# First MLP layer by seven block products for pairs of channel tiles, in a transformer-like layer kernel on one core

## The chip, the core and the metric

The kernel runs on one core of a Trainium2 chip. The core has TensorE for matrix products, VectorE, ScalarE and GpSimd for element-wise work, SyncE that issues the DMAs, an on-chip memory SBUF of 128 partitions and a small accumulator memory PSUM, into which TensorE writes. The engines run their own instruction lists side by side and wait for each other by semaphores. In the rows they are called PE (PEld is its weight load), DVE, ACT, POOL and SP.

The metric is the device time of one launch in microseconds (us). Three runs of the kernel before took 1729.58, 1735.76 and 1736.58 us; the median is 1735.76.

## The reference

One layer on 1024 tokens of width 1024, in float32. The time mixer before it fills the first thousand us and isn't touched. What matters here is the second half:

```python
x = _layernorm(DEEPNORM_ALPHA * x + g1 * mix, ln1_g, ln1_b)
h = _modulate(x, sh2, sc2)                       # layer norm, times (1 + sc2), plus sh2
ff = jnp.square(jax.nn.relu(h @ w_ff1 + b_ff1)) @ w_ff2 + b_ff2     # 1024 -> 4096 -> 1024
return _layernorm(DEEPNORM_ALPHA * x + g2 * ff, ln2_g, ln2_b)
```

To keep float32 accuracy with bf16 matmuls, every operand is split in a high part (its bf16 rounding) and a low part (the residual, rounded). A product is three matmuls: high x high, high x low, low x high.

## The kernel before

The work is written as a chain of stages, each a block with one list per engine and a barrier at its end. Two stages matter.

**The output stage, `phase_out`.** It goes over eight token tiles `t` of 128 tokens. TensorE makes the output projection (`out_products`, L2015), VectorE and ScalarE add the residual and normalise twice, TensorE transposes the result (L2383), ScalarE applies scale and shift by eighths (`piece`, L2271), rounds to `a_hi` (L2275), and GpSimd makes the residual `a_lo` (`low`, L2247). So `a_hi` and `a_lo` hold the input of the MLP with channels on the partitions: 8 channel blocks of 128 by 1024 tokens. For the last tile VectorE does half of the piece (L2367, L2370) and the residual. At the end TensorE already makes the tiles 0 and 1 of the MLP's 4096 hidden channels (`ff_part`, L2206), for the tokens whose pieces are ready; their last 128 tokens wait for the last `a_lo`. The weights of tiles 2 and 3 are loaded and split here too (L150, L154).

**The MLP stage, `phase_mlp`.** The 32 tiles of hidden channels go in 8 groups of four. For a tile TensorE issues 8 channel blocks x 3 matmuls x 2 halves of the tokens, 48 matmuls of 128x512 (`gemm_rows`, L218), into a PSUM tile of 1024 columns. ScalarE takes the relu (L2515), VectorE the square (L2607), ScalarE rounds to `c_hi` (L2519), GpSimd makes `c_lo` (L2552). Beside it the weights of the tile after next are loaded (512 KB), rounded by ScalarE (L2437) and their residual made by GpSimd (L2441). For a group the second layer's weights (2 MB) are loaded, scaled by VectorE (L2599), rounded (L2524) and their residual made (L2557). TensorE's order is: first layer of group i+1, then second layer of group i, 16 outputs of 12 matmuls (`gemm_tokens`, L674), each added by VectorE to the sum in SBUF (L2619). In the last group VectorE and ScalarE normalise what is done. The middle of the stage stands in engine loops (`steps`), each turn of which does two groups. The order on each engine is the order of the code.

Of the kernel before, what the change touches and what calls it, by code (L numbers as in the profile page):

```python
# [7 lines left out]
F32 = mybir.dt.float32  # L8
# [2200 lines left out]

def phase_out(nc, g, a):  # L2210

    with ExitStack() as es:
        sb = lambda n, s=(P, D), d=F32: es.enter_context(nc.sbuf_tensor(f"ou_{n}", list(s), d))
        names = "vec brow mm y s1 v1 sd1 r1 n1 gain bias keep s2 v2 sd2 r2 n2 turn hf hi lo tail_hf tail_hi".split()
# [4 lines left out]
        hf = sb("hf", (P, KT, P))  # L2219
# [5 lines left out]
        turned = [es.enter_context(nc.psum_tensor(f"ou_turned{u}", [P, D], F32)) for u in range(2)]  # L2225
# [7 lines left out]
        load_next, split_next, cut_next, _ = first_weights(nc, "ff1", ff_buffers(g), lambda u, i: [(slice(0, KT), w1[:, :, (2 + u) * P:(3 + u) * P])])  # L2233
        tok = lambda t: slice(t * P, (t + 1) * P)
        inside = lambda t: 0 <= t < TT
        LAST = TT - 1
# [7 lines left out]
        def low(eng, t):  # L2244
            if inside(t):
                wait(eng, t, "hi")
                eng.tensor_tensor(g.a_lo[:, :, tok(t)], hf[:], g.a_hi[:, :, tok(t)], ALU.subtract).then_inc(s["lo"], 1)  # L2247

        @block.sync
        def _(sp):  # L2250
# [7 lines left out]
            wait(sp, LAST, "mm")  # L2258
            load_next(sp)

        @block.scalar
        def _(act):

            def piece(t):
# [23 lines left out]
            for t in range(TT):  # L2288
# [9 lines left out]
                root(t, 1)  # L2298
            second(LAST)
            for u in range(2):  # L2300
                split_next(act, u)
            piece(LAST)

        @block.gpsimd
        def _(pool):
            for t in range(TT):
                low(pool, t - 2)
                if t in SPLIT_AT:
                    cut_early(pool, t - SPLIT_AT[0])
            low(pool, LAST - 1)  # L2310
            for u in range(2):
                cut_next(pool, u)

        @block.vector
        def _(dve):
# [45 lines left out]
            scale(LAST, 1)  # L2361
            keep(LAST)
            wait(dve, LAST, "turn")
            wait(dve, LAST - 1, "lo")
            half = KT // 2
            for kt in range(half, KT):
                dve.tensor_scalar(hf[:, kt, :], turned[LAST % 2][:, kt * P:(kt + 1) * P], g.ada[:, ADA["sc2"] + kt:ADA["sc2"] + kt + 1],  # L2367
                                  g.ada[:, ADA["sh2"] + kt:ADA["sh2"] + kt + 1], ALU.mult, ALU.add).then_inc(s["tail_hf"], 1)
            dve.wait_ge(s["tail_hf"], half)
            dve.tensor_copy(g.a_hi[:, half:KT, tok(LAST)], hf[:, half:KT, :]).then_inc(s["tail_hi"], 1)  # L2370
            dve.wait_ge(s["tail_hi"], 1)
            low(dve, LAST)

        @block.tensor
        def _(pe):
# [33 lines left out]
            ff_part(pe, ps[1], early[1][1], early[2][1], g, HALF, SEQ - P)  # L2409
            wait(pe, LAST, "lo")  # L2410
# [4 lines left out]
def ff_buffers(g):  # L2415

    tile = lambda at: g.z[:, at, :].rearrange("p (k n) -> p k n", n=P)
    part = lambda at, x: g.z[:, at, x * HALF:(x + 1) * HALF].bitcast(BF16).rearrange("p (k n) -> p k n", n=P)
    return [tile(10 + u) for u in range(2)], [part(12 + u, 0) for u in range(2)], [part(12 + u, 1) for u in range(2)]


def ff_weights(nc, g, a):


    ff = Net()
    w1 = a["w_ff1"][0].rearrange("(k p) n -> p k n", p=P)
    stage, ff.hi, ff.lo = ff_buffers(g)
    loaded, hi_ready, ff.lo_ready, ff.used = ([nc.alloc_semaphore(f"ff1_{n}{u}") for u in range(2)] for n in "in hi lo used".split())

    def load(sp, m, u, col):  # L2430
        sp.wait_ge(ff.lo_ready[u], m + 1)
        sp.dma_start(stage[u], w1[:, :, ds(col, P)]).then_inc(loaded[u], 16)

    def split_hi(act, m, u):
        act.wait_ge(loaded[u], (m - 1) * 16)
        act.wait_ge(ff.used[u], m + 1)
        act.activation(ff.hi[u], stage[u], ACT.Copy).then_inc(hi_ready[u], 1)  # L2437

    def split_lo(pool, m, u):
        pool.wait_ge(hi_ready[u], m - 1)  # L2440
        pool.tensor_tensor(ff.lo[u], stage[u], ff.hi[u], ALU.subtract).then_inc(ff.lo_ready[u], 1)  # L2441

    ff.load, ff.split_hi, ff.split_lo = load, split_hi, split_lo
    return ff


def phase_mlp(nc, g, a, out):

    with ExitStack() as es:  # L2452
# [4 lines left out]
        w2 = a["w_ff2"][0].rearrange("(g k p) n -> p (g k) n", p=P, k=GT)  # L2457
        st2 = sb("st2", [P, GT, D])
        hi2, lo2 = ([sb(f"{n}{b}", [P, GT, D], BF16) for b in range(2)] for n in ("hi2_", "lo2_"))
        r = [sb(f"r{u}", [P, SEQ]) for u in range(2)]  # L2460
        ps1 = g.ps
        wide = [es.enter_context(nc.psum_tensor(f"ff_ps2_{u}", [P, D], F32)) for u in range(2)]
        ps2 = [wide[u // 2][:, u % 2 * HALF:(u % 2 + 1) * HALF] for u in range(4)]
        ff = ff_weights(nc, g, a)
        s_used1 = ff.used
# [259 lines left out]
```

## Time and profile before

| what | us |
|---|---|
| median of three runs | 1735.76 |
| span of the profiled execution | 1730.9 |
| runs, lowest and highest | 1729.58, 1736.58 |
| TensorE busy in the span | 1643.6 |
| VectorE, ScalarE, GpSimd busy | 769.0, 562.3, 451.3 |

The profiled execution gives a span, from its first to its last instruction; no device time of its own stands beside it, so the 4.9 us between its span and the median of the runs are taken as what lies around it. A matmul of 128x512 is shown with 0.38 us, but the next one starts before it ends, so a stretch of matmuls is read by its starts. An element-wise operation that is held up while it runs is shown longer: its span holds the wait. In a merged row (x4) the span covers all of them.

### The profile page before, as it was taken

The page shows a single profiled execution, that of the slowest core. Times are in us where ns is not written, and L with a number is a line of the kernel's source. Part 1 is how long each engine was busy: PE and PEld are TensorE (multiplying, and loading weights), DVE is VectorE, ACT ScalarE, POOL GpSimd, SP SyncE. Part 2 cuts the span into 40 slices and gives each one's busy share as a digit, 9 for nine tenths or more (in the row PEclk, how much of TensorE's full clock was granted, in tenths as well). Part 3 has the DMA queues.
Part 4 walks back from the last instruction along what each step waited for, and adds up shares of the span by engine and source line. Part 5 has one row for each costly group of instructions (what it writes and reads, how often), then busy time and mean ns, then how long its engine had stood idle before and what let it go on. Part 6 is the DMA issues. An engine that isn't in the chain of part 4 may idle for free. (4 is left out here: it accounts for less than half of the span.)

```text
span 1730.9 us, 34492 instructions
## 1 busy us (share of the span) xinstructions
PE 1643.6 (95%) x14983; PEld 857.5 (50%) x15178; DVE 769.0 (44%) x1061; ACT 562.3 (32%) x884; POOL 451.3 (26%) x236
## 2 busy tenths in 40 slices
PE   4998999998999998999999999999999999999997
PEld 2444666666545555544444455444444444444443
DVE  5597666666325455313111486433232323232338
ACT  5323544454324555411312165421211212120300
POOL 1231322222110112123422122742323333232310
PEclk9999999999999999999999999999999999999999
DMA  9851001000111200312110311420202021112002
GB/s 354 265 199 41 16 4 39 4 28 28 27 46 28 62 1 1 126 58 61 48 36 25 110 49 47 137 86 25 73 24 73 25 72 36 61 36 85 1 1 97
DMA packets 105773, 109.69 MB, mean 63 GB/s; under 512 B 2592, under 2 KB 82610, under 8 KB 105394
## 3 DMA queue, kind: packets, MB, share of 16 engines
q1 hardware_dynamic: 105648, 107.82, 19.2%
q8 instruction: 103, 1.69, 0.4%
q14 instruction: 22, 0.18, 0.0%
HBM read 101.52 MB, written 4.19 MB: 61 GB/s over the span
## 5 line engine op out<-in xcount | busy, mean ns | idle before, releaser
L218 PE MATMUL tokens_ps<-a_hi,z 128*128 128x512 bf16 x878 | 228.5, 379 | 0.9
L674 PE MATMUL ff_ps<-ff_hi,c_lo 128*128 128x512 bf16 x503 | 190.6, 379 | 0.6
L674 PE MATMUL ff_ps<-ff_hi,c_hi 128*128 128x512 bf16 x501 | 189.9, 379 | 1.4 <-DVE z L2619 0.9
L674 PE MATMUL ff_ps<-ff_lo,c_hi 128*128 128x512 bf16 x501 | 189.9, 379 | 0.6
L2619 DVE TENSOR_TENSOR z<-ff_ps,z 128x512 f32<-128x512 f32 x128 | 88.3, 690 | 205.0 <-PE ff_ps L674 204.3
L2515 ACT ACTIVATE ff_r<-tokens_ps,cols 128x1024 f32<-128x1024 f32 x30 | 33.4, 1114 | 421.4 <-PE tokens_ps L218 414.4
L2441 POOL TENSOR_TENSOR z<-z 128x1024 bf16<-128x1024 f32 x28 | 62.3, 2225 | 345.1 <-ACT z L2437 345.1
L218 PEld LDWEIGHTS tokens_ps<-a_hi,z 128*128 128x128 bf16 x896 | 87.6, 98 | 105.8
L2607 DVE TENSOR_TENSOR ff_r<-ff_r 128x1024 f32<-128x1024 f32 x32 | 41.1, 1284 | 219.2 <-ACT ff_r L2515 219.2
L218 PE MATMUL tokens_ps<-a_lo,z 128*128 128x512 bf16 x438 | 131.1, 379 | 0.5
L195 POOL TENSOR_TENSOR mg_wlo<-mg_stage,mg_whi 128x1024 bf16<-128x1024 f32 x21 | 45.6, 2175 | 149.9 <-ACT mg_whi L191 149.9
L2552 POOL TENSOR_TENSOR c_lo<-ff_r,c_hi 128x1024 bf16<-128x1024 f32 x32 | 75.9, 2371 | 29.4 <-ACT c_hi L2519 29.4
L674 PEld LDWEIGHTS ff_ps<-ff_hi,c_hi 128*128 128x128 bf16 x512 | 50.1, 98 | 61.6 <-issue 1.3
L674 PEld LDWEIGHTS ff_ps<-ff_hi,c_lo 128*128 128x128 bf16 x512 | 50.1, 98 | 60.4
L674 PEld LDWEIGHTS ff_ps<-ff_lo,c_hi 128*128 128x128 bf16 x512 | 50.1, 98 | 60.2
L808 DVE TENSOR_TENSOR_SCAN b_lo<-z,sb_ahead 128x256 f32<-128x256 f32 (+3 forms) x32 | 50.5, 1621 | 46.8 <-ACT z L925 46.8
L218 PEld LDWEIGHTS tokens_ps<-a_lo,z 128*128 128x128 bf16 x448 | 43.8, 98 | 52.9
L2557 POOL TENSOR_TENSOR ff_lo<-ff_st,ff_hi 128x1024 bf16<-128x1024 f32 x32 | 68.1, 2158 | 0.0
L2599 DVE TENSOR_TENSOR ff_st<-ff_st,z 128x1024 f32<-128x1024 f32 x32 | 67.3, 2160 | 1.7 <-DMA ff_st<-w_ff 1.7
L808 DVE TENSOR_TENSOR_SCAN b_hi<-z,sb_ahead 128x128 f32<-128x128 f32 (+3 forms) x32 | 48.3, 1551 | 43.1 <-ACT z L925 43.1
L2169 DVE TENSOR_TENSOR mg_ga<-mg_ga,mg_ps 128x1024 f32<-128x1024 f32 x7 | 8.5, 1221 | 131.6 <-PE mg_ps L218 131.6
L1648 PE MATMUL rw_front<-a_hi,z 128*128 128x512 bf16 x179 | 58.2, 387 | 3.0 <-issue 2.9
(420 smaller groups left out, 3219.2 us busy)
## 6 DMA issues: line engine op xcount, KB each, us to landing
ff_st<-w_ff SPq DMA_DIRECT2D x8, 2048.0 KB, 7.7
z<-w_ff SPq DMA_DIRECT2D x30, 512.0 KB, 4.0
ada_w<-w_ada SPq DMA_DIRECT2D x6, 2048.0 KB, 8.2
z<-w_in SPq DMA_DIRECT2D x18, 512.0 KB, 4.4
z<-w_ada SPq DMA_DIRECT2D x8, 1024.0 KB, 13.5
mg_stage<-w_in SPq DMA_DIRECT2D x16, 512.0 KB, 4.0
zs_stage<-w_in SPq DMA_DIRECT2D x8, 512.0 KB, 8.2
ada_w<-w_ada SPq DMA_DIRECT2D x4, 1024.0 KB, 13.5
```

Of the source, the lines that this page charges most:

```text
L195: pool.tensor_tensor(lo[u][:], stage[u][:], hi[u][:], ALU.subtract).then_inc(lo_ready[u], 1)
L218: last = pe.matmul(out[:, h * HALF:(h + 1) * HALF], w[:, kt, :], a[:, slot, h * HALF:(h + 1) * HALF], start=(x == 0 and y == 0), stop=(x = ...
L674: last = pe.matmul(out, a[:, slot, at], w[:, x, n], start=(x == 0 and y == 0), stop=(x == k - 1 and y == 2))
L808: dve.tensor_tensor_scan(prod[b][:, 0:nk][:, ::-1], m, masked, 1.0, ALU.mult, ALU.max).then_inc(s_scan, 1)
L1648: mm = pe.matmul(unit_bank(u)[:], w_part[:, kt, :], a_part[:, kt, h * HALF:(h + 1) * HALF], start=(x == 0), stop=(x == 3 * KT - 1))
L2441: pool.tensor_tensor(ff.lo[u], stage[u], ff.hi[u], ALU.subtract).then_inc(ff.lo_ready[u], 1)
L2515: act.activation(r[u][:], (wide if begun and t >= begun else ps1)[u][:], ACT.Relu, bias=g.cols[:, ds(gr * GT + (b1 + t), 1)]).then_inc(s_r ...
L2552: pool.tensor_tensor(g.c_lo[:, GT * par + t, :], r[u][:], g.c_hi[:, GT * par + t, :], ALU.subtract).then_inc(s_ulo[u], 1)
L2557: pool.tensor_tensor(lo2[par][:, k, :], st2[:, k, :], hi2[par][:, k, :], ALU.subtract).then_inc(s_o2, 1)
L2599: dve.tensor_tensor(st2[:, k, :], st2[:, k, :], g.g2, ALU.mult).then_inc(s_m2, 1)
L2607: dve.tensor_tensor(r[u][:], r[u][:], r[u][:], ALU.mult).then_inc(s_sq[u], 1)
L2619: dve.tensor_tensor(acc, ps2[x % 4], acc, ALU.add).then_inc(s_acc, 1)
```

## The change

For tile pairs the first layer is a 2x2 block product. The weights of a pair of tiles are split by input channels (blocks 0 to 3, blocks 4 to 7) and by tile, the activations by input channels and by half of the tokens. Instead of eight block products, each of 12 matmuls of 128x512, seven are made (`ff_product`), of sums of blocks on both sides, and the four quarters of the result are sums of the seven products. This holds for the tiles 2 to 31, 15 pairs; tiles 0 and 1 stay as they were.

The sums of activation blocks are made once, at the end of the output stage, on VectorE, from the float32 pieces, which for this are all kept (`piece_of`); they are rounded and split into `b_hi`, `b_lo` (`sums`, `sum_high`, `sum_low`). The sums of weight blocks are made for every pair (`ff_sums`, four additions on VectorE in a 1 MB staging buffer `st1`, of which there is one), after the unsummed blocks have been split from it (`first_high`, `first_low`) and before the summed ones are (`sums_high`, `sums_low`). The sums of products are made by VectorE from PSUM (six additions of 128x512 in `pair`), after ScalarE has copied the first product to SBUF (`u2`); relu, square and the split then go by quarters of 128x512. The products have four banks of PSUM: products 5 and 3 stand where product 1 stood, and 4 where 2 stood, so TensorE waits for the copy or the addition that empties a bank. The second layer's weights now come in halves of 1 MB. Products 1 and 2 of the first pair are made in the output stage. The engine loops are written out.

```diff
+FF_ORDER = (1, 2, 6, 7, 5, 4, 3)
+QUARTERS = ((0, 0), (1, 1), (1, 0), (0, 1))
+def ff_product(pe, g, w, n, out, onto=False):
+    whi, wlo, bhi, blo = ff_operands(g, w)[n]
+    for kt in range(PAIRS):
+        for y, (m, b) in enumerate(((whi, bhi), (whi, blo), (wlo, bhi))):
+            last = pe.matmul(out, m[:, kt, :], b[:, kt, :], ...)
+def ff_sums(eng, st, k):
+    if k == 0:
+        return eng.tensor_tensor(st[:, K1, N1], st[:, K0, N1], st[:, K1, N1], ALU.add)
...
 # output stage, VectorE
             scale(LAST, 1)
+            sums(HT)
             keep(LAST)
+            sums(HT + 1)
+            dve.wait_ge(s["wal"], 2)
+            for k in range(4):
...
+                ff_sums(dve, next_st, k).then_inc(s["ws"], 1)
             wait(dve, LAST, "turn")
...
             low(dve, LAST)
+            sums(HT + 2)
+            sums(LAST)
+            for t in range(HT + 1, TT):
+                sum_low(dve, t, 1)
 # output stage, TensorE
             ff_part(pe, ps[1], early[1][1], early[2][1], g, HALF, SEQ - P)
+            for x in range(2):
+                ff_product(pe, g, next_w, FF_ORDER[x], turned[0][:, x * HALF:(x + 1) * HALF]).then_inc(s["ahead"], 1)
             wait(pe, LAST, "lo")
 # MLP stage, VectorE
+            def pair(n, x, banks, late=None):
...
+                dve.tensor_tensor(quarter(0, 0), u2, of(2), ALU.add).then_inc(s_c, 1)
+                product(n, 6)
...
+                dve.tensor_tensor(u2, u2, of(6), ALU.add).then_inc(s_c, 1)
+                square(n, 0)
...
+                dve.tensor_tensor(u3, u2, of(7), ALU.add).then_inc(s_c, 1)
+                if late:
+                    late()
...
+                dve.tensor_tensor(quarter(1, 1), u3, of(5), ALU.add).then_inc(s_c, 1)
+                square(n, 1)
 # MLP stage, TensorE
+            def pair(n, x):
...
+                    if p == 5:
+                        pe.wait_ge(s_p1, n + 1)
+                    if p == 4:
+                        pe.wait_ge(s_c, n * 6 + C11)
+                    if p == 3:
+                        pe.wait_ge(s_c, n * 6 + C22)
```

How the instructions move shows at three places. The first is VectorE at the end of the output stage, before: L2335 stores the last row, L2367 to L2247 are the last piece.

```order
L2335 SCALAR_TENSOR_TENSOR z<-ou_y,ou_vec 128x1024
L2367 TENSOR_SCALAR ou_hf<-ou_turned,ada 128x128 x4
L2370 CAST a_hi<-ou_hf 128x4x128
L2247 TENSOR_TENSOR a_lo<-ou_hf,a_hi 128x8x128
L2212 UNCONDITIONAL_BRANCH
```

The same place of the changed kernel, from the second block of activation sums on (L2438 is the store; a first block of four stands ahead of it; L2264 to L2269 are the weight sums).

```order
L2438 SCALAR_TENSOR_TENSOR z<-ou_y,ou_vec 128x1024
L2444 TENSOR_TENSOR ou_hf<-ou_hf 128x512
L2446 TENSOR_TENSOR ou_hf<-ou_hf,ou_xf 128x512
L2448 TENSOR_TENSOR ou_xf<-ou_hf,ou_xf 128x4x128
L2450 TENSOR_TENSOR ou_xf<-ou_xf 128x4x128
L2264 TENSOR_TENSOR c_hi<-c_hi 128x4x128
L2266 TENSOR_TENSOR c_hi<-c_hi 128x4x128
L2268 TENSOR_TENSOR c_hi<-c_hi 128x4x128
L2269 TENSOR_TENSOR c_hi<-c_hi 128x4x128
L2488 TENSOR_SCALAR ou_x<-ff_wide,ada 128x128 x4
L2491 CAST a_hi<-ou_x 128x4x128
L2314 TENSOR_TENSOR a_lo<-ou_x,a_hi 128x8x128
```

Twelve sums now stand between the last normalisation and the last piece, and behind its residual follow eight more and three residuals of `b_lo`.

The second place is VectorE at the start of the MLP, before: squares and scalings of the first group, up to the start of the engine loop.

```order
L2607 TENSOR_TENSOR ff_r<-ff_r 128x1024 x2
L2599 TENSOR_TENSOR ff_st<-ff_st,z 128x1024 x4
L2607 TENSOR_TENSOR ff_r<-ff_r 128x1024 x2
L2478 UNCONDITIONAL_BRANCH
L2478 ISA
```

And now: L2860 are the squares of tiles 0 and 1, L2803 scalings, L2264 to L2269 weight sums for the second pair, L2830 the addition that frees the bank of product 2, L2814 squares of quarters, L2844 the addition that frees the bank of product 5.

```order
L2860 TENSOR_TENSOR a_hi<-a_hi 128x4x256
L2860 TENSOR_TENSOR a_lo<-a_lo 128x4x256
L2803 TENSOR_TENSOR ff_st<-ff_st,z 128x1024 x2
L2264 TENSOR_TENSOR z<-z 128x4x128
L2266 TENSOR_TENSOR z<-z 128x4x128
L2268 TENSOR_TENSOR z<-z 128x4x128
L2269 TENSOR_TENSOR z<-z 128x4x128
L2830 TENSOR_TENSOR a_hi<-ff_u,ff_wide 128x2x256
L2833 TENSOR_TENSOR ff_u<-ff_u,ff_wide 128x512
L2814 TENSOR_TENSOR a_hi<-a_hi 128x2x256
L2837 TENSOR_TENSOR ff_u<-ff_u,ff_wide 128x512
L2844 TENSOR_TENSOR a_lo<-ff_u,ff_wide 128x2x256
```

The additions on which TensorE waits stand behind scalings and weight sums, and a square stands between them.

The third place is ScalarE between the first and the second pair, which has no like in the kernel before: L2655 rounds the last quarter of the first pair, L2645 a half of the second layer's weights, L2635 to L2640 split the first-layer weights of the third pair, L2660 copies the second pair's first product.

```order
L2655 ACTIVATE c_hi<-a_hi 128x512
L2645 ACTIVATE ff_hi_0<-ff_st 128x1024 x2
L2635 ACTIVATE ff_last<-z 128x512
L2636 ACTIVATE z<-z 128x1024
L2640 ACTIVATE z<-z 128x2048
L2660 ACTIVATE ff_u<-tokens_ps 128x512
```

The copy that frees the bank of the first product stands behind all weight work for the next pair.

## Rows read from the trace of the kernel before

**Rows 1.** The page, busy time of TensorE: us, share, instructions.

```profile
PE 1643.6 (95%) x14983; PEld 857.5 (50%) x15178; DVE 769.0 (44%) x1061; ACT 562.3 (32%) x884; POOL 451.3 (26%) x236
```

**Rows 2.** Windows of the MLP stage, all engines.

```profile
core 0: us, PE busy (x) PEld busy (x) DVE busy (x) ACT busy (x) POOL busy (x), PEclk, DMA share, GB/s
1200.00:1300.00 100.00, 99.47 (x455) 45.35 (x464) 35.24 (x30) 22.49 (x22) 34.01 (x15) 1.00 0.15 48
```

**Rows 3.** TensorE's waits: line, who ended them, us, times, longest.

```profile
PE ff_ps L218 <- POOLq L88: 1.9, 1, 1.9
...
PE tokens_ps L2206 <- DVE a_lo L2247: 1.1, 1, 1.1
...
PE ff_ps L674 <- DVE z L2619: 0.9, 1, 0.9
```

**Rows 4.** Timeline of TensorE in the MLP: start, us, engine, line, operation, idle before.

```profile
1103.33 1.03 PE L218 MATMUL tokens_ps<-a_hi,z 128*128 128x512 bf16 x4
1104.19 0.59 PE L218 MATMUL tokens_ps<-a_lo,z 128*128 128x512 bf16 x2
```

**Rows 5.** Timeline of VectorE, two operations of 128x512.

```profile
961.21 0.69 DVE L2197 TENSOR_TENSOR mg_m<-mg_ga,mg_gb 128x512 f32<-128x512 f32 x1
...
1230.87 0.69 DVE L2619 TENSOR_TENSOR z<-ff_ps,z 128x512 f32<-128x512 f32 x1 [1.90 <-PE ff_ps L674]
```

**Rows 6.** Timeline of ScalarE, rounding of the second layer's weights.

```profile
1226.57 3.88 ACT L2524 ACTIVATE ff_hi<-ff_st 128x1024 bf16<-128x1024 f32 x4
```

**Rows 7.** Timeline of GpSimd in the MLP.

```profile
1229.62 8.40 POOL L2557 TENSOR_TENSOR ff_lo<-ff_st,ff_hi 128x1024 bf16<-128x1024 f32 x4
...
1287.50 2.22 POOL L2441 TENSOR_TENSOR z<-z 128x1024 bf16<-128x1024 f32 x1 [5.97 <-ACT z L2437]
1289.68 3.11 POOL L2552 TENSOR_TENSOR c_lo<-ff_r,c_hi 128x1024 bf16<-128x1024 f32 x1
```

**Rows 8.** Timeline of VectorE in the MLP, squares and scalings.

```profile
1082.16 2.25 DVE L2607 TENSOR_TENSOR ff_r<-ff_r 128x1024 f32<-128x1024 f32 x1 [2.13 <-ACT ff_r L2515]
...
1224.35 1.23 DVE L2607 TENSOR_TENSOR ff_r<-ff_r 128x1024 f32<-128x1024 f32 x1 [9.13 <-ACT ff_r L2515]
...
1287.65 8.49 DVE L2599 TENSOR_TENSOR ff_st<-ff_st,z 128x1024 f32<-128x1024 f32 x4
```

**Rows 9.** Timeline of VectorE at the end of the output stage.

```profile
1065.36 1.21 DVE L2335 SCALAR_TENSOR_TENSOR z<-ou_y,ou_vec 128x1024 f32<-128x1024 f32 x1
1068.28 1.37 DVE L2367 TENSOR_SCALAR ou_hf<-ou_turned,ada 128x128 f32<-128x128 f32 x4 [1.71 <-PE ou_turned L2383]
1069.68 0.47 DVE L2370 CAST a_hi<-ou_hf 128x512 bf16<-128x512 f32 x1
1070.76 2.46 DVE L2247 TENSOR_TENSOR a_lo<-ou_hf,a_hi 128x1024 bf16<-128x1024 f32 x1 [0.61 <-ACT a_hi L2275]
```

**Rows 10.** Timeline of TensorE between the output stage and the MLP.

```profile
1073.28 0.23 PE L2206 MATMUL tokens_ps<-a_hi,c_lo 128*128 128x128 bf16 x1 [1.14 <-DVE a_lo L2247]
...
1075.91 0.22 PE L2206 MATMUL tokens_ps<-a_hi,c_lo 128*128 128x128 bf16 x1
1078.08 0.38 PE L218 MATMUL ff_ps<-a_hi,z 128*128 128x512 bf16 x1 [1.95 <-POOLq L88]
```

**Rows 11.** Timeline of GpSimd at the end of the output stage.

```profile
1067.73 4.40 POOL L154 TENSOR_TENSOR z<-z 128x1024 bf16<-128x1024 f32 x2 [2.32 <-ACT z L150]
```

**Rows 12.** The page, DMA issues: transfer, count, KB each, us to landing.

```profile
ff_st<-w_ff SPq DMA_DIRECT2D x8, 2048.0 KB, 7.7
z<-w_ff SPq DMA_DIRECT2D x30, 512.0 KB, 4.0
```

**Rows 13.** Windows of TensorE behind a long wait: length, busy, clock, DMA share, GB/s.

```profile
676.00:680.00 4.00, 1.66 (x5) 0.54 0.00 0
680.00:684.00 4.00, 4.00 (x16) 0.61 0.00 0
```

**Rows 14.** Timeline of TensorE at the same place: the matmul behind the wait.

```profile
678.34 0.63 PE L894 MATMUL tokens_ps<-a_lo,mg_whi 128*128 128x512 bf16 x1 [5.95 <-POOL mg_wlo L154]
```

More of the change, by code:

```diff
@@ L2224, in phase_out @@
         ps = g.ps
-        turned = [es.enter_context(nc.psum_tensor(f"ou_turned{u}", [P, D], F32)) for u in range(2)]
+        turned = g.wide
         block = es.enter_context(nc.Block())
@@ L2412, in _ @@
                 ff_part(pe, ps[u], early[1][u], early[2][u], g, SEQ - P, SEQ)
[L2415 to L2444, printed above, removed]
 def phase_mlp(nc, g, a, out):
@@ new lines, in high, with pair @@
+            def high(par, x, n, k):
+                t, h = QUARTERS[k]
+                act.wait_ge(s_sq, n * 4 + k + 1)
+                act.activation(pieces(c_at(g.c_hi, par, x, t, h)), quarter(t, h), ACT.Copy).then_inc(s_uhi, 1)
+            def pair(gr, par, x, n, banks, early=None, late=None):
+                act.wait_ge(s_prod, n * NP + 1)
+                act.wait_ge(s_c, n * 6)
+                act.activation(u2, pieces(bank(banks, x, 1) if banks is narrow else banks[0]), ACT.Copy).then_inc(s_p1, 1)
+                for k in range(4):
+                    relu(gr, x, n, k)
+                    if k == 0 and early:
+                        early()
+                    high(par, x, n, k)
+                    if k == 1 and late:
+                        late()
@@ L2538, in _ @@
+            steps(first, step)
             for t in range(TT):
@@ L2543, in _ @@
         def _(pool):
-            credit(pool, ff.lo_ready * 3 + s_ulo + [s_o2])
-            def group(gr, par, last, begun=0):
-                for t in range(GT):
-                    u, m = t % 2, gr * 2 + t // 2
-                    if not (last and t >= 2) and t >= begun:
-                        ff.split_lo(pool, m + 1, u)
-                    pool.wait_ge(s_uhi[u], m + 1)
-                    pool.tensor_tensor(g.c_lo[:, GT * par + t, :], r[u][:], g.c_hi[:, GT * par + t, :], ALU.subtract).then_inc(s_ulo[u], 1)
@@ L2570, in _ @@
+            steps(first, step)
         @block.vector
@@ new lines, in first, with step, late @@
+            def first():
+                for t in range(2):
+                    dve.wait_ge(s_frelu, t + 1)
+                    dve.tensor_tensor(r[t], r[t], r[t], ALU.mult).then_inc(s_fsq, 1)
+                scale2(0, 0)
+                for k in range(4):
+                    sums(2, k)
+                pair(0, 1, ps2)
+                scale2(0, 1)
+                for k in range(4):
+                    sums(3, k)
+            def step(i, par, last, more):
+                gr = i + 1
+                if not last:
+                    scale2(gr, 0)
+                    pair(gr * 2 - 1, 0, narrow)
+                    scale2(gr, 1)
+                    def late():
+                        if more:
+                            for k in range(4):
+                                sums(gr * 2 + 2, k)
+                    pair(gr * 2, 1, narrow, late)
@@ L2621, in step @@
                         norm(t, h, i * NO + x + 2)
+                    if more and 6 <= x < 10:
+                        sums(gr * 2 + 3, x - 6)
                 if last:
@@ L2650, in second, with step @@
                                 slice(h * HALF, (h + 1) * HALF), range(GT * par, GT * par + GT)).then_inc(s_mm2, 1)
-            def step(i, par, last):
+            def step(i, par, last, more):
                 if not last:
-                    group(i + 1)
+                    pair((i + 1) * 2 - 1, 0)
+                    pair((i + 1) * 2, 1)
                 second(i, par)
-            steps(pe, lambda: group(0, 2), step)
+            steps(first, step)
 def setup(nc, es):
```

423 lines of the change are left out of this document (318 added, 105 removed).

## The prediction

> **What bounds the kernel now.** I read the page's busy shares first, then the windows, then TensorE's waits, then the timelines of the places that the change touches. TensorE is busy 95% of the span [rows 1]. In the MLP stage it is busy 99.5 of every 100 us at full clock, VectorE 35, ScalarE 22, GpSimd 34 [rows 2]. Its waits there sum to 3.9 us: 1.9 behind the barrier between the output stage and the MLP, 1.1 for the last a_lo of VectorE, 0.9 in the MLP [rows 3]. So the MLP is a dense stream of matmuls, and what counts is their start-to-start time, not the 0.38 us that one takes: four starts lie between 1103.33 and 1104.19, 0.2155 us each [rows 4]. Sums are made against this execution (span 1730.9 us) and moved to the median of the runs, 1735.8, by adding the 4.9 us between them.
>
> **What goes.** Tiles 0 and 1 stay as they are. For each of the other 15 pairs the first layer issued 96 matmuls; seven block products of 12 are 84. The instruction lists agree: 180 matmuls fewer. 180 x 0.2155 = **38.8 us less**, if the rest keeps up. A pair now takes 7 x 2.59 = 18.1 us of TensorE in place of 20.7.
>
> **What is added, and its prices.** Per pair VectorE gets six additions with one operand in PSUM (0.69 each, priced by the L2619 row), four sums of weight blocks (0.69, priced by L2197 [rows 5]), and four squares of half width for two of 1.23. ScalarE gets a copy of the first product and copies of 512 and 2048 columns (I take 0.6 and 1.9, since a run of four 1024-wide ones takes 3.88 [rows 6]). GpSimd makes the same residuals (2.1 per 1024 columns, four in 8.40 [rows 7]) in other sizes: 1.07, 2.12 and 4.2. By sums alone this fits.
>
> What does not fit so easily is that VectorE and GpSimd stop each other. GpSimd took the residual at 1287.50; VectorE's four scalings, issued at 1287.65, took 8.49 us where free operations of this width take 1.23 each, 4.9, and GpSimd's next residual, 1289.68, took 3.11 in place of 2.12 [rows 7, 8]. The additions from PSUM show none of it: 0.69 at 1230.87, in the middle of GpSimd's run of four [rows 5, 7]. So I count: an operation of VectorE with two inputs in SBUF (squares, scalings, weight sums, block sums of the activations, residuals) waits for the GpSimd operation under way, up to 1.9 us behind a 1024-wide one, up to 4 behind a 2048-wide one, and the other way round 1.0; then the two alternate. Each holds the other off some 0.1 to 0.2 us less than its own span, else the 8.49 would be 9.1 (2.07 + 1.23 + 2.12 + 3 x 1.23).
>
> The Trainium skill, "SBUF — State Buffer", "Who interferes with whom", calls this an exclusive lock between a VectorE operation with two SBUF inputs and a GpSimd operation that reads SBUF, held for the whole instruction. By that rule, the trace agrees on who waits; on how long, its 8.49 is a little short of the whole-instruction count. What the whole-instruction hold would do here is the second rival.
>
> **Step A, the end of the output stage.** In the trace VectorE stores the last row at 1065.36, waits for the last transposes until 1068.28, makes its half of the last activation piece and its residual, done 1073.22; TensorE goes on at 1073.28, ends at 1076.13, and starts the MLP at 1078.08, 1.95 later [rows 9, 10]. Now twelve sums of 0.69 stand ahead of that piece (8.3 us, plus the store 1.2: 1074.9), while GpSimd has four 2.12 residuals running; three meetings of about 1.4 make it 1079. Piece and cast, 1.9: 1081. At that moment GpSimd starts the 2048-wide residual (before it was two 1024-wide ones, 4.40, out of VectorE's way [rows 11]), so the last a_lo waits and ends at 1086. Behind it stand eight more sums (5.7), three residuals (3.5) and two meetings (3.8): VectorE is through at 1099. The barrier adds 1.95: TensorE starts the MLP at 1101. It has done two products ahead (5.2). Loss: 1101 - 1078.1 - 5.2 = **17.7 us**. Bounds: 6.8 without any meeting, 20 with whole-instruction holds.
>
> **Step B, the first pair.** Counted from TensorE's start at 1101. The products 6, 7 and 5 end at 7.8. Product 4 writes the bank that holds product 2, so it waits for the first addition, which stands on VectorE behind two squares, two scalings and four weight sums. Those need a 1 MB load (between 4.0 for 512 KB and 7.7 for 2 MB [rows 12]; I take 4.7), two copies (1.7) and two residuals (3.2). From 5 to 20 GpSimd has d_lo, a_lo, two c_lo and two second-layer residuals in a row, 11.7 us, with VectorE's two scalings and first three sums each one behind a GpSimd operation. The first addition comes at 20.5, product 4 at 21.2: **13.4 lost**. Product 3 accumulates onto product 5's bank and waits until the fourth addition has read it; ahead of that is a square that meets the 4.2 us residual of the weight sums: **5.0 lost**. Bounds for both: 6.6 and 20.
>
> **Step C, the second pair.** TensorE has products 1, 2, 6, 7 done at 41.9. Product 5 waits until ScalarE has copied product 1 out, and on ScalarE this copy stands behind all of the weight work for the third pair. That has one staging buffer, which is free at 27, and ScalarE comes to it only behind the first pair and the second-layer copies, at 39; then copies 1.7, four GpSimd operations to 46, four sums 2.8, the 1.9 copy, the copy itself: 50.8. **9.0 lost** (bounds 8 to 10).
>
> **Step D, the third pair.** Four weight sums stand inside the chain of additions, behind two residuals that start after the first addition; **4.1 lost** (bounds 1.8 to 6).
>
> **Step E, groups after that, six of them.** The two pairs take 36.2 us of TensorE. In that time the shared port is wanted for 8 x 1.07 + 4 x 2.12 + 7.4 = 24.5 us by GpSimd and 8 x 0.69 + 4 x 1.23 + 4 x 0.69 = 13.2 by VectorE: 37.7, just over 36.2. The rest of the group, 41.4 us of second layer, wants little of it and takes what is late. I put 0.4 per group, **2.5** (bounds 0 and 14, 2.4 in each group).
>
> **The clock.** Behind a wait of 5.95 us the granted clock was 0.54 in one window of 4 us and 0.61 in the next [rows 13, 14], so mostly at 1.2 GHz in place of 2.4. Five gaps of 4 to 13 us come in here; after most of them TensorE soon waits again, which hides it. **1.0** (0 to 4).
>
> **The sum.** 17.7 + 13.4 + 5.0 + 9.0 + 4.1 + 2.5 + 1.0 = 52.7 lost against 38.8 gained: **13.9 us slower**, 1735.8 + 13.9 = **1750 us** (span 1745). The low bounds give 23.2 - 38.8 = -15.6, the high ones 20 + 20 + 10 + 6 + 14 + 4 - 38.8 = +35.
>
> The written-out stage itself I price at nothing: TensorE waits at no loop end now [rows 2, 3].
>
> **Rivals.** *First: the meetings cost next to nothing and the change is faster.* If the block sums and half-width squares pass GpSimd as the PSUM additions do, VectorE is done with the output stage at 1088, the first pair loses 6.6, the second 8, the third 1.8: 15.6 us faster, 1720. It decides when the meetings in steps A and B fall below about a third of what I count. Against it: the scalings and one square, 2.25 at 1082.16 in place of 1.23, met GpSimd and waited [rows 8]. Chance 0.08.
>
> *Second: meetings cost their whole instruction, and the port is the bound in every group.* With full holds my count of steps A to E becomes 20, 20, 11, 5 and 6 x 1.5 to 2, with the clock's 1.0 a loss of 66 to 69 against 38.8: 27 to 30 slower, 1763 to 1766. For it: the 37.7 against 36.2. Against it: 8.49 and not 9.1. Chance 0.20.
>
> *Third: the start costs only half.* GpSimd's small operations fall between VectorE's and the two engines catch up ahead of the barrier; steps A to C lose 30 to 36 us and not 45: 1735 to 1741, no difference. Chance 0.17.
>
> **How the numbers follow.** The forecast has 0.55, with 1744 to 1758 as its own range. Less than 0.5%, 8.7 us, can't be told from no change. Slower by more than that are the forecast and the second rival: 0.75. Same is the third: 0.17. Faster 0.08. The range of 8 in 10 takes nearly all of the third and nearly all of the second: 1736 to 1770.
>
> **What the profile would show.** Right: TensorE's first MLP matmul 20 us or more later than 1078 while its matmul count falls by 180; a wait of 10 to 16 us of TensorE for an addition of VectorE (products 4 and 3 of the first pair), one of about 9 for ScalarE's copy of product 1, and no wait above 2.5 us from the third group on; weight sums of VectorE with a mean over 1 us, PSUM additions at 0.69. Wrong: means of 0.7 on all VectorE operations (the first rival), or a TensorE wait of 2 us in every group (the second), or VectorE through with the output stage before 1092.

## The result: 18 us slower, and the profile after

The changed kernel takes 1751.28 us (median of 4 runs, 1750.81 to 1754.47), the kernel before 1733.33 beside it (4 runs): a ratio of 1.0105, interval 1.009 to 1.0121, which is 15.6 to 21 us. The spans of the two profiled executions differ by the same 18.0, 1748.9 against 1730.9.

The page of the changed kernel: busy time, and its granted clock in 40 slices, in tenths of full speed:

```profile
PE 1615.1 (92%) x14807; PEld 841.4 (48%) x14998; DVE 920.6 (53%) x1260; ACT 615.6 (35%) x982; POOL 518.5 (30%) x286
...
PEclk9999999999999999999999998689999999999999
```

TensorE has 180 weight loads fewer than in [rows 1] and 28.5 us less of busy time, and still the span grew. Three slices, from 1049 to 1181 us, read 8, 6 and 8 and show where. TensorE's waits (who ended them, total, times, longest):

```profile
PE ff_wide L2242 <- DVE a_hi L2830: 13.8, 1, 13.8
PE tokens_ps L2206 <- DVE a_lo L2314: 10.7, 1, 10.7
PE ff_wide L2242 <- PEq L2994: 9.7, 1, 9.7
PE tokens_ps L2242 <- ACT ff_u L2660: 7.7, 1, 7.7
PE tokens_ps L2242 <- DVE a_lo L2844: 3.5, 6, 2.0
PE ff_wide L2242 <- DVE a_lo L2844: 2.7, 1, 2.7
PE ff_wide L674 <- DVE z L2886: 0.9, 1, 0.9
```

In [rows 3] there were three waits with 3.9 us in all; now they sum to 49. All but 2.4 of it lies ahead of the fourth pair. The same waits in the timeline of TensorE, with the place where each ends (the last row is product 3 of the third pair):

```profile
1085.88 0.29 PE L2206 MATMUL tokens_ps<-a_hi,c_lo 128*128 128x128 bf16 x1 [10.66 <-DVE a_lo L2314]
1100.35 0.63 PE L2242 MATMUL ff_wide<-b_lo,z 128*128 128x512 bf16 x1 [9.66 <-PEq L2994]
1123.53 0.61 PE L2242 MATMUL ff_wide<-b_hi,ff_last 128*128 128x512 bf16 x1 [13.82 <-DVE a_hi L2830]
1130.95 0.61 PE L2242 MATMUL ff_wide<-a_hi,z 128*128 128x512 bf16 x1 [2.69 <-DVE a_lo L2844]
...
1153.49 0.61 PE L2242 MATMUL tokens_ps<-b_hi,ff_wsh 128*128 128x512 bf16 x1 [7.74 <-ACT ff_u L2660]
...
1181.31 0.39 PE L2242 MATMUL tokens_ps<-a_hi,z 128*128 128x512 bf16 x1 [1.99 <-DVE a_lo L2844]
```

Matmuls of 512 columns behind a long wait take 0.61 to 0.63 and not 0.38, and their starts lie 0.43 apart and not 0.216. The windows show the clock there and in the middle of the stage:

```profile
1100.00:1104.00 4.00, 3.65 (x10) 1.41 (x12) 2.36 (x2) 2.56 (x3) 0.00 (x0) 0.54 0.77 242
...
1124.00:1128.00 4.00, 4.00 (x12) 1.36 (x10) 2.81 (x2) 1.43 (x2) 3.10 (x1) 0.55 0.51 208
...
1200.00:1300.00 100.00, 99.09 (x452) 44.83 (x460) 48.17 (x60) 24.42 (x30) 40.35 (x21) 1.00 0.14 46
```

Behind a wait the granted clock is near the lower level, 1.2 GHz. From 1200 on TensorE is almost as dense as in [rows 2], but not quite: 99.1 of 100 us in place of 99.5, and 460 weight loads in place of 464. The difference is a short stop at two places of each group, of which the list of waits shows one with 0.3:

```profile
1260.49 0.38 PE L2242 MATMUL tokens_ps<-b_hi,ff_last 128*128 128x512 bf16 x1
1261.18 0.39 PE L2242 MATMUL tokens_ps<-a_hi,z 128*128 128x512 bf16 x1 [0.31 <-DVE a_lo L2844]
...
1273.92 0.38 PE L674 MATMUL ff_wide<-ff_hi,c_lo 128*128 128x512 bf16 x1
1274.37 0.39 PE L674 MATMUL ff_wide<-ff_hi,c_hi 128*128 128x512 bf16 x1
```

Counted by starts, which should be 0.216 apart, these are 0.47 and 0.23 us.

VectorE at the end of the output stage, which answers to [rows 9]:

```profile
1066.03 3.15 DVE L2438 SCALAR_TENSOR_TENSOR z<-ou_y,ou_vec 128x1024 f32<-128x1024 f32 x1
1069.11 2.61 DVE L2444 TENSOR_TENSOR ou_hf<-ou_hf 128x512 f32<-128x512 f32 x1
1071.76 0.69 DVE L2446 TENSOR_TENSOR ou_hf<-ou_hf,ou_xf 128x512 f32<-128x512 f32 x1
...
1073.82 2.62 DVE L2264 TENSOR_TENSOR c_hi<-c_hi 128x512 f32<-128x512 f32 x1
...
1082.80 3.02 DVE L2314 TENSOR_TENSOR a_lo<-ou_x,a_hi 128x1024 bf16<-128x1024 f32 x1 [2.46 <-ACT a_hi L2351]
...
1093.24 5.41 DVE L2320 TENSOR_TENSOR b_lo<-ou_xf,b_hi 128x1024 bf16<-128x1024 f32 x3
```

Free, such operations take 0.69 and 1.2; here one in every few takes 1.9 more. GpSimd's rows of the same stretch show what was under way each time:

```profile
1065.89 2.21 POOL L2320 TENSOR_TENSOR b_lo<-ou_hf,b_hi 128x1024 bf16<-128x1024 f32 x1 [2.58 <-ACT b_hi L2357]
1068.06 3.11 POOL L2320 TENSOR_TENSOR b_lo<-ou_xf,b_hi 128x1024 bf16<-128x1024 f32 x1
1073.68 2.21 POOL L2320 TENSOR_TENSOR b_lo<-ou_hf,b_hi 128x1024 bf16<-128x1024 f32 x1 [2.50 <-ACT b_hi L2357]
1080.69 4.06 POOL L2413 TENSOR_TENSOR z<-c_hi,z 128x2048 bf16<-128x2048 f32 x1 [4.81 <-ACT z L2392]
```

In the MLP's start it is the same, and the additions from PSUM are spared:

```profile
1117.13 2.49 DVE L2266 TENSOR_TENSOR z<-z 128x512 f32<-128x512 f32 x1
1119.66 2.49 DVE L2268 TENSOR_TENSOR z<-z 128x512 f32<-128x512 f32 x1
1122.19 0.69 DVE L2269 TENSOR_TENSOR z<-z 128x512 f32<-128x512 f32 x1
1122.80 0.68 DVE L2830 TENSOR_TENSOR a_hi<-ff_u,ff_wide 128x512 f32<-128x512 f32 x1
1123.59 0.69 DVE L2833 TENSOR_TENSOR ff_u<-ff_u,ff_wide 128x512 f32<-128x512 f32 x1
1125.46 4.04 DVE L2814 TENSOR_TENSOR a_hi<-a_hi 128x512 f32<-128x512 f32 x1 [1.19 <-ACT a_hi L2650]
```

The square of 4.04 stands beside GpSimd's residual of the weight sums:

```profile
1124.90 4.06 POOL L2725 TENSOR_TENSOR ff_wsl<-z,ff_wsh 128x2048 bf16<-128x2048 f32 x1 [3.29 <-ACT ff_wsh L2640]
```

**A mark for comparing profiles.** The stages ahead of the change end at another time in every execution. VectorE's last row statistics, before and then after:

```profile
1063.21 0.21 DVE L2321 BATCH_NORM_AGGREGATE ou_mv<-ou_st 128x2 f32<-128x12 f32 x1
```

```profile
1061.11 0.21 DVE L2424 BATCH_NORM_AGGREGATE ou_mv<-ou_st 128x2 f32<-128x12 f32 x1
```

So I count single profiles from this mark. From it the kernel before starts the MLP after 14.9 us and ends after 667.7; the changed one after 39.2 and 687.8, 20.1 later. In the eleven profiles of this case the mark lies between 1060.4 and 1068.3. The 20.1 of this pair of profiles is 2 us more than the 18.0 of the medians; why isn't shown, and the table below goes by the profiles.

### The profile page after: what moved, and what is told of

Read it like the earlier page. It is cut to its first block and busy times, and to the rows that moved or that the text cites. A ratio compares the mean times of both kernels' runs of the same rounds, so it can differ in the third digit from the quotient of the medians.

```text
span 1748.9 us, 34071 instructions
## 1 busy us (share of the span) xinstructions
PE 1615.1 (92%) x14807; PEld 841.4 (48%) x14998; DVE 920.6 (53%) x1260; ACT 615.6 (35%) x982; POOL 518.5 (30%) x286
## 5 line engine op out<-in xcount | busy, mean ns | idle before, releaser
L674 PE MATMUL ff_wide<-ff_hi,c_hi 128*128 128x512 bf16 x502 | 190.3, 379 | 1.8 <-DVE z L2886 0.9
L674 PE MATMUL ff_wide<-ff_lo,c_hi 128*128 128x512 bf16 x502 | 190.3, 379 | 0.5
L674 PE MATMUL ff_wide<-ff_hi,c_lo 128*128 128x512 bf16 x501 | 189.9, 379 | 0.5
L2886 DVE TENSOR_TENSOR z<-ff_wide,z 128x512 f32<-128x512 f32 x128 | 86.6, 687 | 150.6 <-PE ff_wide L674 150.6
L674 PEld LDWEIGHTS ff_wide<-ff_hi,c_hi 128*128 128x128 bf16 x512 | 50.1, 98 | 64.0 <-DVE z L2886 2.8
L674 PEld LDWEIGHTS ff_wide<-ff_hi,c_lo 128*128 128x128 bf16 x512 | 50.1, 98 | 60.4
L674 PEld LDWEIGHTS ff_wide<-ff_lo,c_hi 128*128 128x128 bf16 x512 | 50.1, 98 | 59.9 <-issue 0.3
L2814 DVE TENSOR_TENSOR a_lo<-a_lo 128x512 f32<-128x512 f32 x30 | 34.8, 1161 | 46.6 <-ACT a_lo L2650 46.6
L834 PE MATMUL tokens_ps<-a_hi,z 128*128 128x512 bf16 x177 | 56.3, 383 | 0.3
L2242 PE MATMUL tokens_ps<-a_hi,z 128*128 128x512 bf16 x166 | 53.1, 387 | 3.6 <-DVE a_lo L2844 3.5
L2814 DVE TENSOR_TENSOR a_hi<-a_hi 128x512 f32<-128x512 f32 x30 | 44.6, 1485 | 13.0 <-ACT a_hi L2650 13.0
L2803 DVE TENSOR_TENSOR ff_st<-ff_st,z 128x1024 f32<-128x1024 f32 x32 | 47.6, 1528 | 6.7 <-DMA ff_st<-w_ff 6.7
L2242 PE MATMUL tokens_ps<-b_hi,z 128*128 128x512 bf16 x164 | 50.2, 379 | 0.3
## 6 DMA issues: line engine op xcount, KB each, us to landing
z<-w_ada SPq DMA_DIRECT2D x8, 1024.0 KB, 13.4
```

What stands on the lines that cost most here:

```text
L674: last = pe.matmul(out, a[:, slot, at], w[:, x, n], start=(x == 0 and y == 0), stop=(x == k - 1 and y == 2))
L834: mm = pe.matmul(out, w_part[:, kt, :], a_part[:, kt, h * HALF:(h + 1) * HALF], start=(kt == 0 and y == 0), stop=(kt == KT - 1 and y == 2))
L2242: last = pe.matmul(out, m[:, kt, :], b[:, kt, :], start=(kt == 0 and y == 0 and not onto), stop=(kt == PAIRS - 1 and y == 2), skip_group_c ...
L2803: dve.tensor_tensor(st2[:, k, :], st2[:, k, :], g.g2, ALU.mult).then_inc(s_m2, 1)
L2814: dve.tensor_tensor(quarter(*QUARTERS[k]), quarter(*QUARTERS[k]), quarter(*QUARTERS[k]), ALU.mult).then_inc(s_sq, 1)
L2886: dve.tensor_tensor(acc, ps2[x % 4], acc, ALU.add).then_inc(s_acc, 1)
```

## The experiments

Timed ratios are to the kernel before on the same chip; the changed kernel has 1.0105.

**1. The stage written out, alone.**

```diff
-            with eng.Fori(0, (NGR - 2) // 2) as r_:
+            for r_ in range((NGR - 2) // 2):
...
-            with sp.Fori(1, NGR) as gr:
+            for gr in range(1, NGR):
```

> The kernel before, with the two engine loops of the MLP stage written out and nothing else changed. My theory: the written-out stage is free, 0 us against the kernel before (within 2), and all of the 18 us come from waits less the removed matmuls. Rival: some of the time is the longer program (some 2 us of the 18 stand in no wait of TensorE that I can name), then this kernel is 2 us or more slower than the one before.

1.0004 (0.9995 to 1.0014); from the mark 668.0 against 667.7. The written-out stage costs nothing that can be measured.

**2. TensorE kept at work in its waits.** The diff shows one of four places.

```diff
+                        for _ in range(55):
+                            pe.matmul(narrow[0], sets[1].a_hi[:, 0, :], g.b_hi[:, 0, 0:HALF], start=True, stop=True)
                         pe.wait_ge(s_c, C11)
```

> The changed kernel with TensorE kept at work inside its four long waits: matmuls whose results nobody reads, into banks that are free there (150 of 128 columns before the last a_lo, 38 of 512 before the barrier, 55 before product 4 of the first pair, 30 before product 5 of the second). In the changed kernel the granted clock is 0.5 to 0.75 in most windows between 1080 and 1160, and the matmuls between the waits take 8 us longer than at full clock. My theory: those 8 us are hidden, since each stretch ends in a wait for an engine that does not care about TensorE's clock; only the slow matmuls behind the last wait (1181 to 1188, 1.7 us) count, so the gain is 1 to 3 us against the changed kernel (1748 to 1750), and the waits for products 4, 3 and 5 end at the same times. Rival: the low clock costs what it stretches, and the gain is 8 to 10 us (1741 to 1743).

1.0124 (1.0099 to 1.0149), from the mark 688.3: no gain at all, not even my 1 to 3. From the MLP's start on TensorE ran at full clock everywhere but at product 3's wait and the third pair's and behind them, and only came earlier to the same waits:

```profile
PE tokens_ps L2242 <- DVE a_lo L2848: 5.8, 7, 3.8
PE ff_wide L2242 <- DVE a_lo L2848: 4.7, 1, 4.7
```

Product 3 of the first pair now waits 4.7 in place of 2.7, that of the third 3.8 in place of 2.0. In the changed kernel, then, what slow matmuls take is given back by the wait behind them. The matmuls behind the last wait stayed slow, since I had put none there:

```profile
1184.00:1188.00 4.00, 4.00 (x10) 0.50 0.00 0
```

So whether those few can be gained wasn't tried.

**3. Residuals of the output stage on VectorE.**

```diff
-            pool.tensor_tensor(next_w.s_lo, next_st, next_w.s_hi, ALU.subtract).then_inc(s["wsl"], 1)
-            sum_low(pool, HT + 2, 0)
-            sum_low(pool, LAST, 0)
...
+            dve.tensor_tensor(next_w.s_lo, next_st, next_w.s_hi, ALU.subtract).then_inc(s["wsl"], 1)
```

> The changed kernel with the residuals behind the last row of the output stage (five of 1024 columns and the 2048-wide one of the weight sums) taken from GpSimd and given to VectorE. My theory: the two engines take turns at a port for nearly whole instructions, so what GpSimd does in 2.1 us costs VectorE that much of waiting, and doing it itself in 1.2 is cheaper: TensorE starts the MLP about 2 us earlier (1098 in place of 1100.35), and the kernel is 0 to 3 us faster than the changed one although VectorE has 8.4 us more work. No operation of VectorE there takes over its free time (0.69, 1.23). Rival: the engines run side by side and VectorE's long operations have another cause; then 8.4 us more work on the engine that ends last make the start 6 to 8 us later, 1757 to 1759.

1.0082 (1.0065 to 1.0099). The MLP starts 35.3 after the mark, 4.0 earlier, and the end comes 4.8 earlier, with 8.4 us more work on the engine that ends last. That is more than the 0 to 3 that I had expected. VectorE's rows, with GpSimd silent:

```profile
1067.11 1.22 DVE L2431 SCALAR_TENSOR_TENSOR z<-ou_y,ou_vec 128x1024 f32<-128x1024 f32 x1
1068.24 0.68 DVE L2437 TENSOR_TENSOR ou_hf<-ou_hf 128x512 f32<-128x512 f32 x1
...
1084.26 2.28 DVE L2492 TENSOR_TENSOR z<-c_hi,z 128x2048 bf16<-128x2048 f32 x1
```

No row in the stretch is over its free time, the store (3.15 before) included. That settles it against engines that run side by side without stopping each other.

**4. ScalarE's copy first.**

```diff
                 second_high(0, 0, 1)
+                act.wait_ge(s_prod, NP + 1)
+                act.wait_ge(s_c, 6)
+                act.activation(u2, pieces(bank(narrow, 0, 1)), ACT.Copy).then_inc(s_p1, 1)
                 first_high(3, sets[1], True)
```

> The changed kernel with ScalarE's copy of the second pair's first product moved ahead of the weight work for the third pair (step C). My theory: the wait of product 5 (7.7 us) goes, but VectorE comes to the second pair only behind the weight sums of the third pair and the scalings, at 1153.5, so product 4 waits for its first addition in its place: no change in time (within 1 us of the changed kernel), with a wait of 5 to 8 us on an addition of VectorE. Rival: the copy was all that was late, and the kernel gains the 7.7 us, 1743 to 1744.

1.0118 (1.01 to 1.0135), from the mark 688.6: no gain. The wait of product 5 is gone, and this row is new:

```profile
PE tokens_ps L2242 <- DVE a_hi L2834: 5.6, 1, 5.6
```

The copy was the last thing that product 5 waited for, not the thing that was late.

**5. The 2048-wide residual in four pieces**, in the MLP (shown) and at the end of the output stage.

```diff
-                pool.tensor_tensor(w.s_lo, st1, w.s_hi, ALU.subtract).then_inc(s_wsl, 1)
+                for k in range(4):
+                    r = slice(2 * k, 2 * k + 2)
+                    last = pool.tensor_tensor(w.s_lo[:, r], st1[:, r], w.s_hi[:, r], ALU.subtract)
+                last.then_inc(s_wsl, 1)
```

> The changed kernel with the 2048-wide residuals of the weight sums on GpSimd cut into four of 512 columns (at the end of the output stage and in the MLP stage), the same work in shorter instructions. My theory: VectorE is stopped by the instruction under way, so its longest waits shrink with it: the square that took 4.04 in the first pair takes under 1.9, the wait of product 3 (2.7 us) and the one in the third pair (2.0) go or nearly go, and with the time that the later sums gain the kernel is 2 to 5 us faster than the changed one (1746 to 1749). Rival: what stops VectorE is GpSimd's traffic, however it is cut; then the same bytes cost the same and the time stays at 1751 (within 1).

1.0086 (1.0069 to 1.0103), 4 us faster than the changed kernel. The MLP starts 38.8 after the mark and not 39.2, so the gain lies in the MLP. GpSimd's four pieces and the square behind the first of them:

```profile
1128.03 4.95 POOL L2729 TENSOR_TENSOR ff_wsl<-z,ff_wsh 128x512 bf16<-128x512 f32 x4 [3.29 <-ACT ff_wsh L2642]
```

```profile
1128.59 1.14 DVE L2819 TENSOR_TENSOR a_hi<-a_hi 128x512 f32<-128x512 f32 x1 [1.19 <-ACT a_hi L2652]
```

The square went from 4.04 to 1.14 and product 3's wait is gone; GpSimd paid 0.9 us for it. So what stops VectorE there is the instruction under way, and not GpSimd's traffic however it is cut. The third pair's wait stayed (1.8), against what I expected, and product 5 waits 9.7, 2 longer.

**6. Another order at the start of the MLP.**

```diff
                     if p == 4:
-                        pe.wait_ge(s_c, C11)
+                        pe.wait_ge(s_frelu, 2)
                     if p == 3:
-                        pe.wait_ge(s_c, C22)
-                    ff_product(pe, g, sets[1], p, bank(ps2, 0, p), p == 3).then_inc(s_prod, 1)
+                        ff_product(pe, g, sets[1], 5, narrow[3], False)
+                    ff_product(pe, g, sets[1], p, {4: narrow[2], 3: narrow[3]}.get(p, bank(ps2, 0, p)), p == 3).then_inc(s_prod, 1)
...
 # VectorE
-                scale2(0, 0)
                 for k in range(4):
                     sums(2, k)
                 pair(0, 1, ps2)
-                scale2(0, 1)
-                for k in range(4):
-                    sums(3, k)
+                scale2(0, 0)
...
```

> The changed kernel with only the start of the MLP stage put in another order: products 4 and 3 of the first pair go to two banks that are free (product 5 is made a second time for it, 12 more matmuls, 2.6 us), VectorE makes the weight sums ahead of the scalings of the second layer, ScalarE copies the second pair's first product ahead of the third pair's weight work, and the second-layer work and weight sums for the group after move under the second-layer matmuls of the first group. My theory: steps B to D cost 26.5 us of waits and 8 us of half-speed matmuls between them, 34 in all, because of the order in which VectorE, ScalarE and GpSimd come to things; in this order only the chain of the weight sums is left (load 5, copies 1.7, residuals 3.3, sums 2.8, copy 1.9, residual 4.1, against 18.1 us per pair of TensorE), seen as a wait of 5 to 9 us ahead of product 6 of the second and of the third pair. The kernel is 13 to 18 us faster than the changed one: 1733 to 1738. Rival: the waits only change place, as in the copy's run, and the gain is under 5 us: 1746 or more.

1.0033 (1.0021 to 1.0046), 1737.27 us: 14 faster than the changed kernel, from the mark 671.9, 15.9 less.

```profile
PE tokens_ps L2242 <- DVE a_hi L2892: 11.9, 2, 7.2
```

Two waits ahead of product 6 are left, 7.2 and 4.7, where waits and slow matmuls took 34.

**7 and 8. All of it together, without and with matmuls before the barrier.** Kernel 8 has in addition:

```diff
+            for _ in range(50):
+                pe.matmul(turned[1][:, 0:HALF], early[1][0][:, 0, :], g.a_hi[:, 0, 0:HALF], start=True, stop=True)
```

> All that the runs have shown at once: the order of the MLP start of the run before, all residuals behind the last row of the output stage on VectorE, with the last piece ahead of the second half of the sums and the store of the last row behind them, and the weight sums' residual of GpSimd in pieces of 512 columns in the MLP. My theory: the starts' costs add up, so another 5 us at the output stage (TensorE starts the MLP at 1095 or 1096 in place of 1100) and 3 to 5 in the MLP: 1725 to 1730, 3 to 8 us faster than the kernel before (ratio 0.995 to 0.998). Here no wait hides the low clock at the start of the MLP, so some 2 us of it count. Rival: the start's work is bound by VectorE's total, and what I move ahead comes back later: 1733 or more, no faster than the kernel before.

> The kernel of the run before with 50 matmuls of 512 columns, whose results nobody reads, on TensorE between its last matmul of the output stage and the barrier (some 11 us of waiting). In the changed kernel such matmuls gained nothing, by my theory because a wait for VectorE followed each slow stretch. Here no long wait follows, so by the same theory they gain now: the MLP's first 5 us run at full clock, 1.5 to 3 us faster than without them. Rival: they gain nothing here either, because the clock isn't what counts there (within 0.5 us).

Kernel 7: 1731.43 us, 0.999 (0.998 to 0.9999). Kernel 8: 1728.76, 0.9982 (0.9972 to 0.9992), 22.5 faster than the changed kernel and 4 faster than the one before. Both start the MLP 32.9 after the mark. Kernel 7 misses its 1725 to 1730: the start of the MLP came 6 us earlier than in run 6, as hoped, but from there to the end it takes 632.2 in place of 633.0, and not the 3 to 5 less that I had expected. In the third pair GpSimd's residual is now what TensorE waits for, 5.6 in place of the 4.7 for VectorE. Kernel 8 is 2.7 faster than kernel 7 by the medians, but their intervals overlap, and what I gave as the reason for a gain isn't there. Product 4 starts 9.5 us after the MLP's first matmul in both; of the 3.1 by which the profiles differ, 2.3 stand in three later waits, which the added matmuls don't touch. The MLP's first window of kernel 8 is at the lower clock all the same, since the barrier still made TensorE wait 5.3:

```profile
1095.00:1099.00 4.00, 2.58 (x7) 0.94 (x8) 1.07 (x2) 2.60 (x3) 0.00 (x0) 0.50 0.39 108
```

**9. Without the block sums of the activations.**

```diff
-            sums(HT)
             keep(LAST)
-            sums(HT + 1)
...
-            sums(HT + 2)
-            sums(LAST)
```

> The changed kernel without the block sums of the activations: the sixteen sums of the output stage, their eight copies to bf16 and their eight residuals are left out, and the products 4 to 7 read what lay in those tiles before; the weight sums and the whole MLP stage stay as they are. My theory: step A is these sums and the residuals behind them, with VectorE and GpSimd in each other's way, and nothing else; counted from the last row's statistics TensorE starts the MLP 20 us later (14.9 of the kernel before and 5.2 for the two products made ahead) and not 39.2, and the waits of steps B and C stay at 13.8 and 7.7. The kernel is 17 to 20 us faster than the changed one, 1731 to 1734, level with the one before. Rival: half of step A is something else, the four weight sums and their 2048-wide residual or the changed order of TensorE's last matmuls; then the gain is 8 to 12 us, 1739 or more.

This kernel leaves out the sums, so its result is wrong and only its time counts. 1731.29 us, 0.9984 (0.9973 to 0.9995), 20 faster than the changed kernel. The MLP starts 18.1 after the mark, 21.1 earlier. I had expected a start at 20: the two products made ahead also fill the wait for the last `a_lo` ([rows 10], 1.14), and of the 1.95 at the barrier 1.29 are left. The waits of steps B and C stay:

```profile
PE ff_wide L2242 <- DVE a_hi L2815: 15.4, 1, 15.4
PE tokens_ps L2242 <- ACT ff_u L2645: 7.4, 1, 7.4
```

Product 4 waits 1.6 longer than 13.8, because the three products ahead of it run at full clock here.

## Why the prediction was right, step by step

The forecast, 1750, and its chain of reasons held: the matmuls went as counted, the start costs more than they give, later groups cost little. The size of the loss was underrated, and that the time is right to 1.3 us is luck. The step between the kernels is 18.0 (15.6 to 21) and not 13.9; the median of three runs that it was added to, 1735.8, was 2.4 over the 1733.3 of four, and the kernel before took 1732.7 to 1734.7 beside the later runs.

In the timeline each stretch between two starts holds a known number of products of 2.59 us at full clock. What is over is the step's loss, wait and slow matmuls together:

| step | predicted | measured | from |
|---|---|---|---|
| A | 17.7 | 19.2 | 39.2 - 14.9 - 5.2 |
| B | 18.4 | 20.3 | 1100.35 to 1130.95, four products |
| C | 9.0 | 9.6 | to 1153.49, five products |
| D | 4.1 | 4.5 | to 1181.31, nine products |
| E and clock | 3.5 | 5.3 | the rest |
| sum | 52.7 | 58.9 | 20.1 + 38.8 |

**Step A.** The mechanism held: the last `a_lo` was done at 1085.8 (forecast 1086), VectorE at 1098.65 (forecast 1099), but this execution passed the mark 2.1 earlier than that of the kernel before, from which the forecast was counted, so the step is longer than the clock times say. What I mis-sized is the price of a meeting. I had counted three ahead of the last piece, of 1.4 each, and there are three: the store L2438, 3.15 in place of 1.21, and the sums L2444 and L2264, 2.61 and 2.62 in place of 0.69. They cost 1.9 each, 5.8 in place of 4.2, which is about the 1.5 by which the step was set too small. Which operations they would hit I hadn't said; the store, priced at its free 1.2, is one. Run 3 shows it at 1.22 with GpSimd silent. The last `a_lo` was also held 2.46 by ScalarE, whose 2048-wide copy stands ahead of its piece. That isn't in the forecast, and cost nothing here, since GpSimd's residual (to 1084.75) lasted longer. Run 9 says what the block sums cost in all: 21.1.

**Step B.** The first addition came 22.4 after TensorE's start, forecast 20.5: three sums took 2.5 to 2.6 each, as counted, but the loads came later than the 4.7 that I took. ScalarE could begin with the weights 6.1 after TensorE's start, and VectorE with its two scalings 8.6 after it:

```profile
1106.48 0.63 ACT L2635 ACTIVATE ff_wd<-z 128x512 bf16<-128x512 f32 x1 [3.92 <-DMA z<-w_ff]
```

```profile
1108.96 5.62 DVE L2803 TENSOR_TENSOR ff_st<-ff_st,z 128x1024 f32<-128x1024 f32 x2 [5.01 <-DMA ff_st<-w_ff]
```

Product 4 waited 13.8 (forecast 13.4), product 3 2.7 (forecast 5.0), the rest of the 20.3 are slow matmuls. Where run 2 brought TensorE to product 3 at full clock, it waited 4.7. The named cause of product 3's wait, a square behind the 2048-wide residual, is in the rows (4.04), and run 5 takes both away.

**Step C.** The wait is for ScalarE's copy, as said, 7.7 (forecast 9.0). But run 4 shows that the copy's place is not what costs: VectorE is as late. I had named the last link that holds TensorE, not the chain. The forecast's own terms, from 46 on, add up to 51.3 and not to 50.8.

**Step D.** 2.0 of wait and 2.5 of slow matmuls against 4.1; with TensorE warm, in run 2, the wait alone is 3.8.

**Step E.** The groups behind it lose 0.7 each at the two places shown above (1261 and 1274): the addition L2844 stands behind four weight sums, as in step D, and the second is a wait for VectorE's addition L2886 of the second layer, which comes behind a square of 3.10 at 1270.62. Five groups have it, 3.5 in all, against 2.5 forecast (six of 0.4).

**The rivals and the signs.** The second rival has 1.5 to 2 in each group, so a port that bounds every group is out. So is the first rival, since the stops are there and go where GpSimd is silent (run 3), and the third, since steps A to C cost 49 and not 30 to 36. One sign named ahead, "weight sums of VectorE with a mean over 1 us", was wrong for the stage as a whole. Two of the four, grouped by line over the MLP stage (count, busy, mean ns, idle before):

```profile
L2264 DVE TENSOR_TENSOR z<-z 128x512 f32<-128x512 f32 x14 | 17.2, 1225 | 10.8 <-POOL z L2721 7.3 <-POOL ff_wa L2721 3.5
L2268 DVE TENSOR_TENSOR z<-z 128x512 f32<-128x512 f32 x14 | 11.4, 816 | 0.3
```

Only the first of four is over 1 us. In the first pair three of four were stopped, later none but the first of four, as the 1.63 of L2264 at 1256.72.

**The clock.** I put 1.0 for it. The matmuls of steps B to D took some 8 us longer than at full clock (the measured losses less their waits of 26.2), but run 2 gives none of it back. Each slow stretch ends in a wait for an engine that goes by its own time, so what the clock takes the wait gives back. That is the reason given ahead, and it held. What counts is what lies behind the last long wait: product 3 of the third pair took 4.29 (1181.31 to 1185.60) in place of 2.59, 1.7. With the 3.5 of step E that makes 5.2 of the 5.3.

**The hold.** The Trainium skill, "SBUF — State Buffer", "Who interferes with whom", has the two engines exclude each other by a lock. With that, run 5 (GpSimd's instructions shorter, the square 1.14 in place of 4.04) and run 3 (GpSimd silent, the store 1.22 in place of 3.15) agree; how long the hold is to the tenth of a microsecond they don't tell.

What stays open: the 2 us between the profiles' 20.1 and the medians' 18.0, whether kernel 8 is faster than kernel 7 in truth and by what, and whether the 1.7 of slow matmuls behind the last wait can be had back.

## What to carry to other kernels

When matmuls are traded for sums, count the first use, not the average: in the middle of the stage the 38.8 us came in but for 3.5, and the start, where sums, residuals and loads stand in one chain ahead of TensorE, took 54. A helper engine that stops the main one costs it nearly the helper's own, slower duration (1.9 us for a residual of 2.1): at a point where both end on the critical path, the faster one alone is quicker (run 3), and where both must work, short instructions stop less (run 5). And a wait's last releaser is not its cause: before moving it ahead, ask when the next one in the chain would have been ready (run 4).

## What was not expected of the hardware

- VectorE's scalar_tensor_tensor is stopped as well, however narrow: the store of 128x1024 took 3.15 against 1.21 in [rows 9] and 1.22 in run 3, and one of 128x1 took 1.46 beside GpSimd's residual and 0.16 away from it (L2433).
- Four GpSimd residuals of 512 columns took 4.95 where one of 2048 took 4.06, with VectorE taking turns.
- The time at which the untouched first thousand us end differs by up to 8 us between executions (the mark at 1060.4 and at 1068.3), so that profiles are compared from a mark inside.
